# A delta-rule scan in 64x64 blocks on quarters of TensorE, its inverse interleaved with the preceding tile's states

## What the kernel computes

```
def step(S, inp):
    r_t, w_t, k_t, v_t, kk_t, b_t = inp
    sa = jnp.einsum('bhvk,bhk->bhv', S, -kk_t)
    S = S * w_t[:, :, None, :] + sa[..., None] * b_t[:, :, None, :] + v_t[..., None] * k_t[:, :, None, :]
    return S, jnp.einsum('bhvk,bhk->bhv', S, r_t)
```

## Time and profile before

| | us |
|---|---|
| median of 3 runs | 2242.23 (2241.44 to 2248.2) |
| the profiled execution's own time | 2251.15 |
| its span | 2249.4 |
| TensorE busy | 2023.5 (90%) |
| VectorE busy | 1656.6 (74%) |
| ScalarE busy | 774.8 (34%) |
| GpSimd busy | 568.1 (25%) |

### The profile page before, as it was taken

One profiled execution on the slowest core, in us unless ns is written; L12 is line 12 of the kernel. 1 busy time (PEld: TensorE's weight loads), 2 busy tenths in 40 slices (PEclk: granted clock), 3 DMA queues, 4 the chain that ended last, 5 costly groups with the idle time before them and its releaser, 6 DMA issues. The chain is left out here.

```text
span 2249.4 us, 29972 instructions
## 1 busy us (share of the span) xinstructions
PE 2023.5 (90%) x11234; PEld 1735.1 (77%) x11234; DVE 1656.6 (74%) x2848; ACT 774.8 (34%) x1122; POOL 568.1 (25%) x381
## 2 busy tenths in 40 slices
PE   5889997879999997999949999957999999999995
PEld 4879784468888445999949999946888888999994
DVE  5388973144443525999969999957888887999998
ACT  3223544422222003343324555523333333333331
POOL 2322340000000003555420010011222223566561
PEclk9989997869999998999979999978999999999998
DMA  3212230010000403444435767569999998999993
GB/s 124 75 39 75 77 125 15 0 39 1 1 1 11 177 0 136 140 136 131 147 123 205 248 226 242 190 226 321 352 363 355 348 359 300 372 388 389 372 353 122
DMA packets 169672, 410.77 MB, mean 183 GB/s; under 512 B 13505, under 2 KB 85185, under 8 KB 166353
## 3 DMA queue, kind: packets, MB, share of 16 engines
q1 hardware_dynamic: 117712, 253.41, 33.1%
q0 software_dynamic: 36864, 134.23, 16.0%
q10 hardware_dynamic: 14976, 21.50, 2.6%
HBM read 360.33 MB, written 48.76 MB: 182 GB/s over the span
## 5 line engine op out<-in xcount | busy, mean ns | idle before, releaser
L1990 PE MATMUL ps<-v_hl,coef_hl 128*128 128x512 f32 x2304 | 534.9, 392 | 40.1 <-DVE coef_hl L2024 40.1
L1990 PEld LDWEIGHTS ps<-v_hl,coef_hl 128*128 128x128 f32 x2304 | 434.6, 189 | 129.9 <-DVE coef_hl L2024 40.7
L1595 PE MATMUL ps<-h_hl,w_hl 128*128 128x384 f32 (+1 forms) x1664 | 329.2, 350 | 8.7 <-DVE h_hl L1667 8.7
L1595 PEld LDWEIGHTS ps<-h_hl,w_hl 128*128 128x128 f32 x1664 | 295.9, 191 | 20.1 <-issue 9.1
L1807 POOL DMA_INDIRECT gathered_rows<-in_u_rows,pick_index x128 | 134.8, 1053 | 612.9 <-DVE pick_hidden L1817 500.2
L1934 ACT ACTIVATE v_hl<-v_staged 128x1024 fp32r<-128x1024 f32 x128 | 135.3, 1057 | 239.3 <-PE ps L1990 208.5
L1807 POOL DMA_INDIRECT gathered_rows<-in_v,pick_index x128 | 179.1, 1399 | 114.9 <-DVE h_tok L1826 83.0
L2029 DVE TENSOR_TENSOR v_hl<-v_staged,v_hl 128x1024 fp32r<-128x1024 f32 x128 | 156.6, 1223 | 67.6 <-ACT v_hl L1934 67.6
L1496 POOL TENSOR_TENSOR w_hl<-w_staged,w_hl 128x1024 fp32r<-128x1024 f32 x56 | 143.8, 2570 | 152.0 <-ACT w_hl L1521 151.7
L1826 DVE SCALAR_TENSOR_TENSOR h_tok<-gathered_rows,pick_hidden,h_tok 128x1024 f32<-128x1024 f32 x128 | 164.2, 1283 | 10.1 <-DVE h_tok L1826 0.5
L630 PE MATMUL ps<-hT_hl,w_hl 128*128 128x264 f32 (+1 forms) x1024 | 168.7, 323 | 0.0
(11 more groups left out here) (327 smaller groups left out, 2970.5 us busy)
## 6 DMA issues: line engine op xcount, KB each, us to landing
v_staged<-in_v SPq DMA_DIRECT2D x128, 512.0 KB, 8.3
w_staged<-in_stream SPq DMA_DIRECT2D x104, 512.0 KB, 3.9
dense_gates<-lot SPq DMA_DIRECT2D x24, 1024.0 KB, 4.8
gates<-dense_gates SPq DMA_DIRECT2D x16, 1536.0 KB, 13.5
w_staged<-in_w_in_t SPq DMA_DIRECT2D x40, 512.0 KB, 3.5
h1T<-in_stream SPq DMA_DIRECT2D x40, 512.0 KB, 7.0
parked_gelu<-h1T ACTq DMA_DIRECT2D x88, 192.0 KB, 2.8
coef<-parked_gelu SPq DMA_DIRECT2D x88, 192.0 KB, 5.8
```

The lines of the kernel that those rows point to most:

```text
L1595: nc.tensor.matmul(bank, w_hl[:, j % RING, 0, P * k:P * (k + 1)], h_hl[:, part, k, lo:hi], start=(k == 0 and part == 0), stop=False)
L1990: last = nc.tensor.matmul(ps[:, 2 + 2 * t + half, :], coef_hl[:, k % HLS, c, P * t:P * (t + 1)], v_hl[:, k % HLS, v, 512 * half:512 * (hal ...
```

## The change

The stage is rewritten on blocks of 64x64, with the same five tiles.

- **Shapes.** A gram or a step is no longer four products over 128 tokens but eight over 64 (pair `j`, then chunk, innermost), each on a quarter of the array: rows and columns 0 to 63 for the first chunk, 64 to 127 for the second in the steps and in `begin_x`; in the grams the rows are those of `e`, and the columns alternate. `make_u` stays on one quarter for its chunk. In `end_x` the rows alternate with `e`; in `begin_state`, `end_state` and the output of values and updates the columns alternate; in `y_of_state` both. Gram, inverse, power and state buffers hold 64 columns for each block, so that their copies are of 256 elements instead of 512. The two transposes among the steps become products with the identity.
- **Order.** The state chain of tile `tt - 1` is issued in pieces between the steps of tile `tt`, `begin_x` of tile `tt - 1` among the grams; after the last tile its own chain follows. VectorE and ScalarE have their parts of it after fixed entries of `STEPS`. `v_tok`, `inv`, `ak`, `rb` and `rk` are kept for two tiles.
- **Banks.** Transposes, grams and steps now share banks 0 to 2 (before: 4 to 6, 0 to 3, 4 to 7). So the first three gram units wait for ScalarE's copies of the three transposed tensors (values first), and a step's half waits for the copy three halves earlier. x takes banks 3 and 4, u 5, state 6, output 7, each alone.
- **Set-up.** The clearing is gone. The masks are built by GpSimd during `attend`, and copied there into a [128, 7, 64] buffer, the identity among them. Decayed inputs of the next tile are made three entries before a tile's last. Nothing is computed any more from the meta tile's state for its own output.

```diff
+            for m, src in enumerate((*whole, ident)):
+                for x in range(2):
+                    rows = slice(CHUNK * x, CHUNK * (x + 1))
+                    order.put(nc.gpsimd.tensor_copy(masks[rows, m, :], src[rows, rows]))
...
-        v_tok = sb("v_tok", [P, 512])
-        grams = {n: sb(n, [P, 2, 4, P]) for n in ("low16", "low32", "low64", "up16", "inv", "rb", "ak", "rk")}
-        pw = [sb(f"pw{i}", [P, 2, 4, P]) for i in range(4)]
...
+        inv, rb, ak, rk = (sb(n, [P, 2, 2, PAIRS, CHUNK]) for n in ("inv", "rb", "ak", "rk"))
+        pw = [sb(f"pw{i}", [P, 2, PAIRS, CHUNK]) for i in range(4)]
...
+        THROUGH, X, U, S, Y = 3, 3, 5, 6, 7
...
-                for x in (k_tok, b_tok, state):
-                    put(v_.memset(x[:, :, :], 0.0))
-                put(v_.memset(x_sb[:, :], 0.0))
-                put(v_.memset(u_sb[:, :], 0.0))
-                put(v_.memset(v_tok[:, :], 0.0))
...
+                    if i == 0 and tt:
+                        take_x(*past[0])
+                    if i == 3 and tt:
+                        next_state(past[0][0])
+                    if i == 5 and len(past) > 1:
+                        take_x(*past[1])
+                    if i == 8 and len(past) > 1:
+                        next_state(past[1][0])
+                    if i == len(steps) - 3 and tt < NT:
+                        make_hats(tt + 1)
...
+                for i, (dst, bank) in enumerate(((v_tok, 0), (k_tok, 1), (b_tok, 2))):
+                    act.wait_ge(turned, 3 * tt + i + 1)
+                    nc.scalar.activation(dst[0:n, tt % 2, :], ps[0:n, bank, :], ACT.Copy).then_inc(tok_copied, 1)
...
+                    if unit < THROUGH:
+                        pe.wait_ge(tok_copied, 3 * tt + unit + 1)
+                    else:
+                        pe.wait_ge(gram_read, 2 * NG * tt + unit - THROUGH + 1)
...
+                    for j in range(PAIRS):
+                        for c, p0, m in chunks_of(tt):
+                            at = slice(t0 + p0, t0 + p0 + m)
+                            last = mm(ps[p0:p0 + m, unit % THROUGH, HD * j:HD * j + m], lhs[rows, j, at], rhs[rows, j, at],
+                                      start=True, stop=True)
...
+                    for j in range(PAIRS):
+                        for c, p0, m in chunks_of(tt):
+                            rows = slice(p0, p0 + m)
+                            moving = masks[rows, MASK_EYE, 0:m] if rhs is EYE else tile_of(rhs, tt)[rows, e, j, 0:m]
+                            last = mm(ps[rows, (turn_of + 1) % THROUGH, HD * j:HD * j + m], tile_of(lhs, tt)[rows, e, j, 0:m],
+                                      moving, start=True, stop=True)
...
+            def begin_x(tt):
...
+                        for c, p0, m in chunks_of(tt):
+                            rows = slice(p0, p0 + m)
+                            last = mm(ps[rows, X + e, HD * j:HD * (j + 1)], ak[rows, tt % 2, e, j, 0:m],
+                                      v_tok[rows, tt % 2, P * j + HD * e:P * j + HD * (e + 1)],
...
+            def end_x(tt, c, p0, m):
...
+                        last = mm(ps[p0:p0 + m, X + e, HD * j:HD * (j + 1)], aT[rows, j, t0 + p0:t0 + p0 + m],
+                                  state[rows, c % 3, j, :], start=False, stop=(j == PAIRS - 1), skip_group_check=True)
...
+            def make_u(tt, c, p0, m):
...
+                for j in range(PAIRS):
+                    for e in range(2):
+                        last = mm(ps[rows, U, 256 * e + HD * j:256 * e + HD * (j + 1)], inv[rows, tt % 2, e, j, 0:m],
+                                  x_sb[rows, e, j, :], start=True, stop=True, skip_group_check=True)
...
+            def begin_state(tt, c, p0, m):
...
+                        mm(ps[HD * e:HD * (e + 1), S, HD * j:HD * (j + 1)],
+                           k_tok[rows, tt % 2, h], v_tok[rows, tt % 2, h], start=(j == 0), stop=False, skip_group_check=True)
...
+            def end_state(tt, c, p0, m):
...
+                pe.wait_ge(u_read, c + 1)
...
+                        last = mm(ps[HD * e:HD * (e + 1), S, HD * j:HD * (j + 1)],
+                                  b_tok[rows, tt % 2, h], u_sb[rows, e, j, :], start=False, stop=(j == PAIRS - 1),
+                                  skip_group_check=True)
...
+            def y_of_state(tt):
...
+                    for c, p0, m in chunks_of(tt):
+                        for e in range(2):
+                            rows = slice(HD * e, HD * (e + 1))
+                            last = mm(ps[rows, Y, P * j + p0:P * j + p0 + m], state[rows, c % 3, j, :],
+                                      rT[rows, j, t0 + p0:t0 + p0 + m], start=False, stop=False, skip_group_check=True)
...
+            for tt in range(NT + 1):
+                past = chunks_of(tt - 1) if tt else []
+                turn(tt)
+                for i in range(NG):
+                    gram(tt, i)
+                    if i == 2 and tt:
+                        begin_x(tt - 1)
+                for i in range(len(steps_of(tt))):
+                    step(tt, i)
+                    if not tt:
                         continue
+                    if i == 0:
+                        end_x(tt - 1, *past[0])
+                    if i == 1:
+                        make_u(tt - 1, *past[0])
+                    if i == 2:
+                        begin_state(tt - 1, *past[0])
+                        y_of_values(tt - 1, *past[0])
+                    if i == 3:
+                        end_state(tt - 1, *past[0])
+                    if i == 4:
+                        y_of_updates(tt - 1, *past[0])
+                    if tt == 1:
+                        continue
+                    if i == 5:
+                        end_x(tt - 1, *past[1])
...
+            begin_x(NT)
+            begin_state(NT, *first)
+            end_x(NT, *first)
+            y_of_values(NT, *first)
+            make_u(NT, *first)
+            end_state(NT, *first)
+            y_of_updates(NT, *first)
+            end_x(NT, *second)
+            y_of_state(NT)
+            make_u(NT, *second)
+            y_of_values(NT, *second)
+            y_of_updates(NT, *second)
```

More of the change, by code:

```diff
@@ L69 @@
 NPARAM = _n
+MASK_BELOW16, MASK_BELOW32, MASK_BELOW64, MASK_ABOVE16, MASK_ABOVE64, MASK_UPTO64, MASK_EYE = range(7)
 TILES = [(0, META)] + [(META + P * i, P) for i in range(NT)]
@@ L756, in attend @@
         q = p_all[:, CT_Q:CT_Q + 4, 1 + META:PW]
+        ones, masks = g["ones"], g["masks"]
+        whole = [sb(f"mask{n}", [P, P]) for n in range(6)]
+        pool_order = sem("pool_order4")
         blocks = lambda i: list(enumerate(TILES[:i + 2]))
@@ L924, in scan_chunks @@
-        v_tok = sb("v_tok", [P, 512])
-        grams = {n: sb(n, [P, 2, 4, P]) for n in ("low16", "low32", "low64", "up16", "inv", "rb", "ak", "rk")}
-        pw = [sb(f"pw{i}", [P, 2, 4, P]) for i in range(4)]
[L927 to L930, removed]
+        x_sb, u_sb = (scratch[:, 1024 + 512 * x:1536 + 512 * x].rearrange("p (e j t) -> p e j t", e=2, j=PAIRS) for x in range(2))
@@ L978, in before, with steps_before @@
             return sum(2 * sum(s[3] == engine for s in steps_of(i)) for i in range(tt))
+        def steps_before(tt):
+            return 2 * sum(len(steps_of(x)) for x in range(tt))
         def chunks_of(tt):
             return [(0, 0, META)] if tt == 0 else [(2 * tt - 1, 0, CHUNK), (2 * tt, CHUNK, CHUNK)]
[L984 to L1017, removed]
@@ L1019, in _, with tile_of, step_bank, taken_by @@
+        def tile_of(name, tt):
+            return inv[:, tt % 2] if name is INV else name
+        def step_bank(i, e, n, w):
+            return ps[0:n, (2 * i + e + 1) % THROUGH, 0:256].rearrange("p (j t) -> p j t", j=PAIRS)[:, :, 0:w]
+        def taken_by(tt, i, e):
+            who = steps_of(tt)[i][3]
+            n = sum(s[3] == who for s in STEPS[:i + 1])
+            return (step_s if who == "s" else step_v), before(tt, who) + 2 * n - 1 + e
         @block.vector
@@ L1060, in _ @@
-                        dve.sem_inc(gram_read, 1)
+                        unit = 2 * i + e
+                        dve.wait_ge(gram_done, 2 * NG * tt + unit + 1)
+                        bank = ps[0:n, unit % THROUGH, 0:256].rearrange("p (j t) -> p j t", j=PAIRS)[:, :, 0:w]
+                        for dst, m in copies(tt % 2):
+                            last = v_.tensor_tensor(dst[0:n, e, :, 0:w], bank, mask(m), ALU.mult)
+                        if i != 1:
+                            last.then_inc(gram_read, 1)
+                            continue
@@ new lines, in _, with y_part, y_of_values @@
+            parts = [0]
+            def y_part(last):
+                last.then_inc(y_parts, 1)
+                parts[0] += 1
+            def y_of_values(tt, c, p0, m):
+                rows = slice(p0, p0 + m)
+                if parts[0]:
+                    pe.wait_ge(y_parts, parts[0])
+                if tt and p0 == 0:
+                    pe.wait_ge(y_read, tt)
```

(5 more changed lines are left out.)

396 lines of the change are left out of this document (216 added, 180 removed).

## The result

The changed kernel took 2130.88 us (median of 4 runs, 2130.03 to 2135.9) beside 2245.22 for the kernel before (4 runs): a ratio of 0.9496, 95% interval 0.9475 to 0.9517. The forecast was 2155, its range ended at 2133. In a later job the same kernel took 2133.16 (5 runs, 2129.23 to 2140.45), ratio 0.9499 (0.9475 to 0.9523).

What follows compares the result with a forecast made beforehand. Scan tiles were taken as bound by TensorE, half its step work on zeros. 11.5 + 41 + 3 x 37 + 13 + 1.2 + 1.5 = 179.2 us against 265.8, 87 less, gave 2155 us; range 2133 to 2222.

Steps and rivals of the forecast that it cites:

- The stage and its size before: The scan, between barriers in the experts stage, takes 265.8 us; what it saves, the kernel saves.
- The price of a quarter: Steps of the inverse: matmuls on two quarters run together, so a step of 32 takes 0.94 us, not 1.87.
- the page's rule on row tiles and one bank: Steps: quarters run serially, 1.87 us each; 47 us less at 2.4 GHz (chance 0.06), 97 more at 1.2 (0.08).
- that rival: Chain pieces between steps: waits for x and u all stand bare, 45 us a tile, 54 us less; chance 0.06.
- the extra matmuls: 876 matmuls issued a tile where about 460 were; 0.029 us each in a pair, counted as no cost.
- the rival in which it never does: Scan tiles: the clock stays at 1.2 GHz, 54 us a tile, only 21 us less, 2221; chance 0.15.
- The failed step: the clock: Falls to 1.2 GHz among the grams, returns in the steps' first third; 5 us more a tile, 37 in all.
- Tile at full clock: A scan tile of 128 at 2.4 GHz: 8.7 us transposes and grams plus 23.2 steps and pieces, 31.9 us.
- Tile 1: Takes over the first tile's state chain and runs largely at half clock; 41 us in all.
- First tile: Scan's short first tile, its state chain moved into tile 1: 11.5 instead of 28.4 us.
- The end with the step to the next stage: After tile 4 its own chain stands bare, 13 us, then 1.2 us to the next stage.
- The 8.9 us: The median of the runs stands 8.9 us below the profiled execution, so 2164 became 2155.

Runs made afterwards that it cites:

- blocks_only: Changed kernel without the alternation: 64x64 blocks kept, each tile's state chain issued behind its own steps; 2156.75 us, ratio 0.9608 to the kernel before.
- masks_in_scan: Changed kernel with the masks built by GpSimd at the start of the scan instead of in the attention stage; 2145.34 us, ratio 0.9559 to the kernel before.
- beginx_late: Changed kernel with begin_x issued after the last gram instead of among the grams; 2135.93 us, ratio 0.953 to the kernel before.
- before_filled: Kernel before with seven unused 128x128 products in each tile of 128 frames, where TensorE waits between grams; 2243.37 us, ratio 1.0002.

## Why the prediction missed

**Right.** The stage and its size before. The price of a quarter, the term that was to decide: 0.94 forecast, 0.93 measured; the page's rule on row tiles and one bank (the Trainium skill, "TensorEngine Tiling (Array Packing)", "Restrictions and Gotchas"), which would have made it 1.87, does not hold here, where both quarters write one bank on different partitions. The alternation covers all waits for x and u; that rival is out, and blocks_only shows what the scan is without it, 23 us longer. The masks cost the attention stage nothing (masks_in_scan), and the extra matmuls are within the 0.93. The clock returns; the rival in which it never does is out.

**The failed step: the clock.** The prediction took 5 us a tile, "I expect it to return in their first third, as before some 10 us later". It returned 3.4 us after it fell, before the tile's first step (low from 540.4 to 543.8, first step at 544.83), and in tile 4 it did not fall. A low stretch of 3.4 us makes the grams 7.8 us instead of 6.4. That pairing holds in all fifteen tiles of the table's five kernels with unaltered grams: 7.6 to 7.8 in the nine with 3.4 us low, 6.4 in the six with none. So the term was 1.4, 1.4 and 0, not 15 in all: 12 us. Nearly all of that is the length of the low stretches, 6.8 us in three tiles for some 30; the price of one us of low clock, 0.41, is not far from the half that was forecast. What I read wrongly was the table: the 10.2 us of before hold grams of 64 rows on 128 columns for half of their length, and steps behind them; the new tile has other work in that place. Why one kind of stretch lifts the clock and the other does not is not settled, nor why it falls in some tiles and not in others: the changed kernel's tile 4 had no low clock in either trace and the same grams in masks_in_scan had 3.4 us there and none in tiles 2 and 3; beginx_late had 6.8 us in one tile and 3.4 in two with the same order of work. In blocks_only, whose chain stands bare, tiles 2 and 3 had 10 and 21 us of it.

**Smaller terms, all too dear.** Tile at full clock 31.9, measured 29.8 (grams with transposes 7.8 for 8.7, steps with pieces 22.0 for 23.2): 2.1 a tile, 6.3 for three. Tile 1 37.4 for 41. First tile 10.6 for 11.5. The end with the step to the next stage 12.4 for 14.2. The 1.5 us in the next stage can't be seen (all behind 1520.0, before 1522.0). With the clock's 12.2 that makes about 26, from 179.2 to 152.8. The 8.9 us by which the median was put below the profiled execution were rightly taken off: 7.5 of them are most likely (not shown) the long attention stage, which the trace of the kernel before has and most of its runs would not have. The range's low end had allowed full clock in every tile, but left the first tile and a tile at full clock (32 us) as they were in the sum, so it ended 2 us above the result. Of the forecast's 31.9 us, 2.5 were waits between the steps alone; measured, TensorE idles 1.5 us in a whole tile.

## What to carry to other kernels

Count the low clock by what TensorE has to do while it lasts, and let the range reach to no low clock and to slightly less than every term of the sum. Alternating two dependent chains can pay twice, by the waits that it covers and by the clock that it keeps: here in about equal parts, by an estimate. Idle time alone shows too little of the waits; compare the distance from step to step as well. Products added only to keep the clock up gave their gain back here, where they were longer than the wait that they filled. And where a stage has two lengths by itself, a change of a few us needs more traces than one.

## What the runs showed of the hardware

**Two quarters into one bank.** With rows and columns both different, two fp32 matmuls of 64x64 start together: in most steps of the changed kernel 3 to 7 ns apart, and the next pair 51 to 55 ns later. In the step below they are 36 ns apart and the next pair 22 ns later; either way there are two in 58 ns. A whole step, 32 of them, with the last one's tail of 0.22:
```profile
532.50 1.15 PE L1205 MATMUL ps<-masks,inv 64*64 64x64 f32 x32
```

**The attention stage has two lengths.** Nothing in its TensorE work differs between these stretches, first of before, then of the changed kernel, then of the changed kernel again:
```profile
343.90:461.60 117.70, 94.89 (x333) 46.94 (x333) 29.07 (x144) 55.86 (x131) 0.00 (x0) 0.81 0.01 5
```
```profile
346.20:456.30 110.10, 85.38 (x333) 43.41 (x333) 29.01 (x144) 55.23 (x131) 7.46 (x28) 0.91 0.02 5
```
```profile
346.20:463.70 117.50, 92.94 (x333) 46.31 (x333) 29.02 (x145) 55.43 (x131) 7.48 (x28) 0.84 0.02 5
```
333 matmuls, at a mean clock of 0.81 or 0.84 in one length and 0.91 in the other. before_filled, whose attention stage is that of the kernel before, took 110.0; the changed kernel had both. In the twelve traces the stage takes 109.9 to 110.2 us in seven, with 20.5 us of low clock, and 117.4 to 117.7 in five, with 37.5 or 44.4. What decides it is not shown. So 7.5 us come and go in either kernel, with the places where the clock falls: the profiled executions, 120.3 us apart, overstate the change by that, the medians, 114 apart, agree with the scan's 113. The ten runs of before_filled fall into five of 2237.6 to 2239.5 and five of 2247.3 to 2250.0, which fits, but only one of them has a trace.
